# One decoder layer on Trainium2: two token tiles ahead of the expert gathers, the other three beside them

## The reference

```python
mod = silu(c) @ w_ada + b_ada;  sh1, sc1, ga1, sh2, sc2, ga2 = split(mod, 6)
h = rmsnorm(x, g_pre1) * (1 + sc1) + sh1
parts = split(h @ w_in)                      # mLSTM, dilated attention, two gates
branch_a = mlstm(parts, state) @ w_a;  branch_b = attention(parts, caches) @ w_b
merged = sigmoid(parts[14]) * branch_a + sigmoid(parts[15]) * branch_b
x = x + ga1 * rmsnorm(merged @ w_out, g_post1)
h2 = rmsnorm(x, g_pre2) * (1 + sc2) + sh2
q = h2 @ peer_wq                             # 8 heads x 2 halves x 128
# per token and head: top 16 of 128 keys in each half, top 16 of the 256 sums
act = gelu(einsum('td,thkd->thk', h2, u[eidx]))
f = einsum('thk,thkd->td', softmax(sc) * act, v[eidx])   # 16384 experts, rows of 1024
x = x + ga2 * rmsnorm(f, g_post2)
```

## Time and profile before

| | us |
|---|---|
| median of 3 runs | 2613.13 (2599.5 to 2623.63) |
| profiled execution, own time | 2621.62 |
| its span in the profile | 2619.8 |
| TensorE busy | 2230.4 (85%) |
| VectorE busy | 1232.3 (47%) |
| ScalarE busy | 699.8 (27%) |
| GpSimd busy | 733.4 (28%) |
| TensorE clock granted, mean | 0.911 |

### The profile page before, as it was taken

How to read it: one execution, slowest core, us unless ns; L and a number is a source line. 1 busy time by engine, 2 the same in 40 slices (tenths; PEclk the granted TensorE clock), 3 DMA queues, 4 the chain that set the end, 5 groups by cost and what they waited for, 6 DMA issues and landing times.

```text
span 2619.8 us, 24988 instructions
## 1 busy us (share of the span) xinstructions
PE 2230.4 (85%) x9002; PEld 1266.2 (48%) x9002; DVE 1232.3 (47%) x3186; ACT 699.8 (27%) x2118; POOL 733.4 (28%) x694
## 2 busy tenths in 40 slices
PE   6999989988687999988879797978888768687786
PEld 2777438875575777454434343434443323233221
DVE  1000001215223011466766767667676776767764
ACT  2000012232121000233333333333333443333322
POOL 0000001111101000035444353434444444344441
PEclk8999989997676999999999898989999899898889
DMA  6566648978673126089999999999999999999997
GB/s 270 230 256 256 242 144 304 320 288 326 234 263 135 53 73 206 33 331 418 418 417 420 412 420 410 419 405 420 408 417 414 416 420 410 414 415 412 419 414 302
DMA packets 134915, 850.42 MB, mean 325 GB/s; under 512 B 15121, under 2 KB 32817, under 8 KB 52989
## 3 DMA queue, kind: packets, MB, share of 16 engines
q0 software_dynamic: 85760, 691.32, 65.1%
q1 hardware_dynamic: 47740, 154.95, 16.2%
q10 hardware_dynamic: 1290, 2.55, 0.3%
HBM read 836.43 MB, written 99.37 MB: 357 GB/s over the span
## 4 chain that ended last, share of the span: by engine, by line
PE 21%; DVE 17%; DMA 17%; ACT 2%; issue 2%; POOL 1%; ACTq 0%; POOLq 0%
PE ps L1694 17%; DMA pr_ring<-in_uv,pr_idx 17%; DVE pr_ring L1873 4%; PE ps L1643 3%; POOL pr_ring L1602 1%; PE ps L1616 1%; DVE pr_hot L1857 1%; DVE pr_hot L1853 1%; DVE pr_ind L1834 1%; ACT pr_coef L1750 1%; DVE pr_ind L1831 1%; DVE pr_pick L1860 1%; DVE pr_val L1833 1%; DVE pr_rest L1832 1%; DVE pr_val L1830 1%
## 5 line engine op out<-in xcount | busy, mean ns | idle before, releaser
L1694 PE MATMUL ps<-pr_ring,pr_diag 128*128 128x512 f32 (+1 forms) x2304 | 1082.4, 625 | 274.1 <-ACT pr_diag L1754 274.1
L1602 POOL DMA_INDIRECT pr_ring<-in_uv,pr_idx x576 | 661.7, 1149 | 1099.3 <-PE ps L1694 766.0
L1873 DVE CUSTOM_DVE_ANT_0 pr_ring<-pr_ring,h 128x1024 f32<-128x1024 f32 x576 | 690.8, 1224 | 421.5 <-DMA pr_ring<-in_uv,pr_idx 420.2
L1694 PEld LDWEIGHTS ps<-pr_ring,pr_diag 128*128 128x128 f32 (+1 forms) x2304 | 437.5, 195 | 879.9 <-issue 509.2
L1745 ACT ACTIVATE pr_gel<-pr_dots 128x2 f32<-128x2 f32 x288 | 58.3, 202 | 619.1 <-DVE pr_dots L1873 619.0
L1754 ACT ACTIVATE pr_diag<-ident,pr_coef 128x128 f32<-128x128 f32 x512 | 173.5, 386 | 0.0
L1750 ACT ACTIVATE pr_coef<-pr_gel,pr_wgt 128x1 f32<-128x1 f32 x576 | 138.5, 287 | 27.6 <-ACT pr_gel L1745 1.1
L1414 PE MATMUL ps<-trunk,h 128*128 128x288 f32 x512 | 129.5, 413 | 12.6 <-DMA h<-in_w_merge 12.6
L1616 PE MATMUL ps<-trunk,pr_wq 128*128 128x192 f32 (+3 forms) x544 | 131.4, 396 | 0.4 <-ACT trunk L1712 0.4
L430 PE MATMUL ps<-trunk,ap_ring 128*128 128x288 f32 x384 | 126.5, 411 | 2.9 <-PEq L323 2.9
L431 PE MATMUL ps<-trunk,ap_ring 128*128 128x288 f32 x384 | 125.5, 409 | 0.0
(11 more groups left out here) (291 smaller groups left out, 2044.8 us busy)
## 6 DMA issues: line engine op xcount, KB each, us to landing
...
sa_ring<-in_cache SPq DMA_DIRECT2D x24, 1024.0 KB, 7.8
...
sa_ring<-in_kcacheB SPq DMA_DIRECT2D x16, 1024.0 KB, 7.6
...
h<-in_w_merge SPq DMA_DIRECT2D x16, 768.0 KB, 4.3
...
```

The source lines that it names most:

```text
L1602: pool.indirect_dma_start(ring[:, n % RING, :], None, d["uv"], bass.IndirectOffsetOnAxis(ap=idx[:, b % 4, j:j + 1], axis=0)).then_inc(arri ...
L1694: mm = pe.matmul(ps[0:r, bank + half, :], diag[:, n % RING, 0:r], ring[:, n % RING, o:o + CHUNK], start=h == 0 and j == 0, stop=b == FINAL ...
L1873: ins = dve.tensor_tensor_reduce(u, u, e.h2[:, BLOCKS[b][0], :], 1.0, 0.0, ALU.mult, ALU.add, dots[:, n % RING:n % RING + 1])
```

## The change

`merge` now covers only the 256 columns of tiles 0 and 1, and only they are projected, normed and turned ahead of the loop. The 320 columns of tiles 2 to 4 are done inside it: from g = 2 on a unit every three steps (gate, branch, nothing), then eight feature blocks of the output projection, transposed, one every two steps, then 13 steps for each of three tiles (transposes back, the two norms, `turn`). Their weights come a second time, through two slots `side_unit`. The blocks go by two tiles now: tiles 0 and 1 through 8 heads, tiles 2 and 3 through 8 heads, tile 4. So there are 16 rounds of queries, of 256 columns and then of 320, whose weights (1 MB each) have one slot in place of two. The ring of gathers has 8 slots in place of 10.

```diff
-GROUP = 3
+GROUP = 2
 GROUPED = GROUP * P
-BLOCKS = [(i, h) for h in range(PH) for i in range(GROUP)] + [(i, h) for i in range(GROUP, NCH) for h in range(heads_of(i))]
+REST = T - GROUPED
+BLOCKS = ([(i, h) for h in range(PH) for i in range(GROUP)] + [(i, h) for h in range(PH) for i in range(GROUP, PT)]
+          + [(PT, h) for h in range(heads_of(PT))])
...
-QUERY_BANK, SCORE_BANK, SUM_BANK = 0, 1, 2
-
...
+def round_of(b):
+
+    return min(b // 2, ROUNDS - 1)
+
+
+def query_count(r, piece):
+
+    return piece if r == 0 else 4 + 2 * (r - 1) + piece
...
+def query_span(r, piece):
+
+    if r == 0:
+        return slice(piece // 2 * P, (piece // 2 + 1) * P)
+    return slice(0, GROUPED) if r < PH else slice(GROUPED, T)
+
+
...
+def query_piece(g):
+
+    b, q = divmod(g, PER)
+    if b == 0:
+        return (1, q) if q in (0, 1) else None
+    if b > 0 and b % 2 and q in (4, 6) and b // 2 + 2 < ROUNDS:
+        return b // 2 + 2, (q - 4) // 2
+    return None
+
...
-RING = 10
+    sp.dma_start(e.wq[:], d["peer_wq"][h // 2][:, :, o:o + 2 * P]).then_inc(e.wq_ready, 16)
+
+
+def side_merge(g):
+
+    u, step = divmod(g - SIDE_FIRST, 3)
+    return (u, step) if 0 <= u < 2 * KD and step < 2 else None
+
+
+def side_product(g):
+
+    b, step = divmod(g - SIDE_FIRST - 3 * 2 * KD, 2)
+    return b if 0 <= b < KD and step == 0 else None
+
+
+def side_tile(g):
+
+    i, step = divmod(g - SIDE_FIRST - 3 * 2 * KD - 2 * KD, 13)
+    return (i + GROUP, step) if 0 <= i < NCH - GROUP else None
...
+RING = 8
 BATCH = 2
 PER = TOPK // BATCH
+SIDE_FIRST = 2
```

The first gather waits for the two tiles alone, and TensorE's step gets the side work after its values and scores:

```diff
-                        if n == 2:
-                            pool.wait_ge(s_mm, NCH)
-                        if n == 8:
-                            pool.wait_ge(s_h2, NCH)
+                        if n == 0:
+                            pool.wait_ge(s_mm, GROUP)
                         if n >= RING:
                             pool.wait_ge(s_v, n - RING + 1)
...
+                def rest_gate(u):
+                    pe.wait_ge(front.unit_ready[u % 2], 16 * (u // 2 + 1))
+                    if u >= 1:
+                        pe.wait_ge(s_sig, u)
+                    for c in range(KD):
+                        mm = pe.matmul(ps[:, SIDE_BANK, 0:REST], front.unit[:, u % 2, c, :], k.hT[:, c, rest_cols],
+                                       start=c == 0, stop=c == KD - 1)
+                    mm.then_inc(s_gate, 1)
+
+                def rest_branch(u):
+                    if u >= 1:
+                        pe.wait_ge(s_taken, u)
+                    src = k.oaT if u % 2 else k.hmT
+                    for c in range(H):
+                        mm = pe.matmul(ps[:, SIDE_BANK + 1, 0:REST], front.unit[:, u % 2, KD + c, :], src[:, c, rest_cols],
+                                       start=c == 0, stop=c == H - 1)
+                    mm.then_inc(s_branch, 1)
...
@@ -1697,19 +1784,35 @@
                             mm.then_inc(s_v, 1)
                         if q == SCORE and b + 2 < len(BLOCKS):
                             scores(b + 2)
-                        for piece in query_pieces(i, h, q):
-                            query(h + 1, piece)
+                        g = b * PER + q
+                        if query_piece(g):
+                            query(*query_piece(g))
+                        unit = side_merge(g)
+                        if unit and unit[1] == 0:
+                            rest_gate(unit[0])
+                        if unit and unit[1] == 1:
+                            rest_branch(unit[0])
+                        if side_product(g) is not None:
+                            rest_product(side_product(g))
+                        tile = side_tile(g)
+                        if tile and tile[1] == 0:
+                            rest_rows(tile[0])
+                        if tile and tile[1] == 10:
+                            turn(tile[0])
```

SP now walks through the same steps, each load behind the work that frees its slot:

```diff
+                sp.wait_ge(s_q, query_count(1, 0))
+                load_query_weights(sp, d, e, 1)
+                for g in range(PER * FINAL[PT]):
+                    piece = query_piece(g)
+                    if piece and piece[1] == 1 and piece[0] + 1 < ROUNDS:
+                        sp.wait_ge(s_q, query_count(piece[0] + 1, 0))
+                        load_query_weights(sp, d, e, piece[0] + 1)
+                    unit = side_merge(g)
+                    if unit and unit[1] == 1:
+                        u = unit[0] + 2
+                        sp.wait_ge(s_branch, unit[0] + 1)
+                        if u < 2 * KD:
+                            sp.dma_start(front.unit[:, u % 2], d["w_merge"][u]).then_inc(front.unit_ready[u % 2], 16)
+                        else:
+                            sp.dma_start(front.unit[:, u % 2, 0:KD, :], d["w_out_b"][u - 2 * KD]).then_inc(
+                                front.unit_ready[u % 2], 16)
+                    feature = side_product(g)
+                    if feature is not None and feature + 2 < KD:
+                        sp.wait_ge(s_out_mm, feature + 1)
+                        sp.dma_start(front.unit[:, feature % 2, 0:KD, :], d["w_out_b"][feature + 2]).then_inc(
+                            front.unit_ready[feature % 2], 16)
```

```diff
+                def chunk(at):
+                    pe.wait_ge(ready[at], 16)
+                    if at >= 2:
+                        pe.wait_ge(s_part, at - 1)
+                    for step in range(2):
+                        for j in range(4):
+                            c = 2 * j + step
+                            mm = pe.matmul(ps[32 * j:32 * j + 32, at % 2, :], k.cs[:, c, :], w[:, at, c, :],
+                                           start=step == 0, stop=step == 1)
+                    mm.then_inc(s_mm, 1)
+
+                def fold(at):
+                    pe.wait_ge(s_part, at + 1)
+                    for b in range(HALF):
+                        o = (at * HALF + b) * NC
+                        mm = pe.matmul(ps[:, FOLD, o:o + NC], part[:, at, b * P:(b + 1) * P], fold9[:], start=True, stop=True)
+                    mm.then_inc(s_fold, 1)
+
                 pe.wait_ge(s_silu, 1)
-                for w in range(NCK):
-                    pe.wait_ge(ready[w % NR], 16 * (w // NR + 1))
...
+                    for i in range(PT):
+                        pe.transpose(ps[:, TURN + c % 4, i * P:(i + 1) * P], x[:, i, c * P:(c + 1) * P], k.ident[:])
+                    pe.transpose(ps[:, SAMPLE, c * TS:(c + 1) * TS], x[0:TS, PT, c * P:(c + 1) * P],
+                                 k.ident[0:TS, 0:TS]).then_inc(s_tr, 1)
+                pe.wait_ge(s_const, 112)
+                fold(0)
+                fold(1)
+                chunk(2)
+                chunk(3)
+                pe.wait_ge(s_mod, 1)
+                fold(2)
+                fold(3)
 
```

490 lines of the change are left out of this document (266 added, 224 removed).

## The result

| | before | changed |
|---|---|---|
| median, us | 2617.27 (5 runs, 2599.5 to 2623.63) | 2647.46 (5 runs, 2639.13 to 2662.23) |
| ratio | | 1.0161, 95% interval 1.0108 to 1.0214 |
| profiled execution, own time (span) | 2621.62 (2619.8) | 2662.19 (2660.4) |
| TensorE / VectorE busy | 2230.4 / 1232.3 | 2223.2 / 1232.1 |
| clock granted, mean | 0.911 | 0.912 |

What follows compares the result with a forecast made beforehand. TensorE was taken to bound the merge and DMA the expert loop. Terms -145 + 69 + 24 + 27 + 27 + 11 gave +13 us on the profiled 2621.6 us, carried to the median as 2626 us; range 2555 to 2690.

Steps and rivals of the forecast that it cites:

- the gains: All terms ahead of the expert loop (first stage, merge, start of the loop) taken together: -145 us.
- First stage: Start of the kernel: inputs load first, matmuls go side by side, attention begins about 43 us: -19 us (-15 to -24).
- Merge: Ahead of the loop: fewer records of 256 columns per unit, load only just covered: -102 us (-95 to -103).
- Start of the loop: From merge to block 1: first gather goes out earlier, but TensorE waits for query weights: -24 us (-14 to -32).
- Side steps: Loop steps with merge and product work, 7.25 blocks: TensorE becomes the bound, 50.5 us a block: +69 us (+57 to +87).
- The three tiles: Norms and turns of three tiles in the loop, 39 steps: ring stall, queries and VectorE work: +24 us (+11 to +45).
- Ring of 8: Loop to the end of block 33: first gather behind a routing lands 1.3 us late each block: +27 us (0 to +60).
- Query rounds: Eight rounds in odd blocks behind the side work: step 6's query delays a gather, 3.3 us each: +27 us (+10 to +40).
- their weights: Loop: 15 loads of 1 MB query weights where there were 6, 2.5 us each if DMA is full: +11 us (+8 to +20).
- Rival A: Loop: DMA hides nearly all of the added work, faster at 2554 us; chance 0.28.
- Rival B: Loop: only seven gathers under way after each routing, queue empties, 4 us a block, 2708 us; chance 0.29.
- Rival C: Side work: table switches and in-order waits of ScalarE and VectorE show, 42 us on top, 2668 us; chance 0.05.

Runs made afterwards that it cites:

- e3: Kernel before with only the new first stage (modulation in column form, input loads first): 2600.8 us, ratio 0.996 to before.
- e6: Changed kernel with the two queries of a round in steps 2 and 4 instead of 4 and 6: 2621.9 us, ratio 1.005 to before.
- e12: e10 plus round 1's query weights in ring slot 9 and a tile's mean one step later: 2551.2 us, ratio 0.977 to before.
- e10: e9 with the first two loads of side weights issued later, behind the keys: 2566.1 us, ratio 0.982 to before.
- e4: Changed kernel with half of the side work's matmuls left out, all loads kept: 2649.2 us, ratio 1.016 to before.
- e7: Changed kernel without the side weight loads behind the first two units, all matmuls kept: 2645.0 us, ratio 1.012 to before.
- e8: Changed kernel with both half of the side matmuls and the later side weight loads left out: 2622.9 us, ratio 1.003 to before.
- e2: Changed kernel with ten ring slots again instead of eight: 2579.3 us, ratio 0.987 to before.
- e1: Kernel before with one change, gathers going round 8 slots instead of 10: 2712.9 us, ratio 1.040 to before.
- e9: Changed kernel with ten ring slots and the queries moved to steps 2 and 4: 2568.2 us, ratio 0.983 to before.

## Why the prediction came out as it did

The predicted 2626 us lies 21 below the median of 2647.5; the gains were 9 us smaller than the sum said at block 1 (136 for 145), and the costs behind it 18 larger (176 for 158). By the spans, the side steps were put 12 us too high, the three tiles 12 too low, and ring, queries and weights together 19 too low (65 for 84). That the misses partly cancel, and that the median falls 2.5 us inside the forecast's own range, is in part luck. The largest single miss is the ring.

- **First stage, -19:** the mechanism was right; the attention started at 50.16 and not near 43, -11.6, and e3 confirms -12. In e6 and e12, whose transposes ran at the pace of TensorE's upper clock, it started at 43.2 and 42.6. The lead's other 6.5 us are not the change's: kernels with this same first stage had the merge's first load anywhere from 808 to 839 us.
- **Merge, -102:** right. From the first gate to the first product less its wait, 832.05 to 917.12, it takes 85.1 us against the 87 worked out.
- **Start of the loop, -24:** too much by 10. What the step left out was a queue it moved work into: SP issues two more loads of weights at the end of the merge, they take 13.31 us to issue, and TensorE cannot begin the next part before. e10 gives 12.7 us back in the front. So the first gather went out at 977 and not near 965. The landing of round 1's weights was sized well: issued at 994.17, used at 1005.43, 11 us against 10.
- **Side steps, +69 (bounds 57 and 87):** the lower bound was the answer, 48.9 us a block. TensorE was the bound as predicted, at 198 of 200 us and clock 0.99, but DMA stood 1 us below it (e4, e7, e8), so the 50.5 for two near-full engines meeting was not needed. With ten slots it is 48.2.
- **The three tiles, +24:** blocks 8 to 13 cost 35.6, of which the ring accounts for 13 to 16 (e2, e1) where I had counted 1.3 a block, and the place of the queries for 8.8 (e6). What is left, 10 to 14 us, no run takes apart.
- **Ring of 8, +27:** this term was mis-sized, and it explains most of the rest. The 1.3 us for the first gather behind a stall came out on average (blocks 8 to 33 of e1). What failed is what the term put at nothing, the gathers behind it. They are issued some 2 us apart with one or two others under way, and six of them lose another 1.8 us. By the length of the blocks e1 measures 2.4 to 3.0 us, a little less than the two together, since a block of the kernel before already takes 40.9 us where 16 x 2.49 is 39.8. For the 20 blocks 14 to 33 it gives +48.8 where 1.3 gave 26. Why the rate of 2.49 us does not come back at once, the runs do not show. In the side steps I had counted nothing for the ring, nearly rightly: ten slots take 4.5 us from blocks 1 to 7 (e2), though e1, with no side work to hide it, pays 21.
- **Query rounds, +27, and their weights, +11:** right in size, wrong in place, and bound to the ring of 8 (with ten slots the move is worth nothing, e9). With the ring's part taken off by e1, blocks 14 to 27 hold 30.4 us of queries and weights for seven rounds, 4.3 each; predicted 3.3 and part of 11 us in all. The odd blocks were to be longer; it is the even ones (47 against 43), since the delayed gathers belong to the next block's dots.
- **Rival A** (DMA hides nearly all) is out: its point of decision, a landing within 5 us on an idle queue, is missed by e1's 6.1. **Rival B** (the ring runs dry) had the better size for the ring, 2.4 to 3.0 measured of its 4 us a block: the late blocks came out at 43.7, near its 44, the DMA share at 0.96, below its 0.97, and its condition, 1.8 us a block, is met. The total stayed nearer to the forecast than to B's 2708. Over blocks 8 to 33 e1 gives 65 us for the ring, where B had 103 and the forecast 34, and the side steps took 12 us less than either had. I had given the forecast 1.3 because the trace of before showed the two landings of 5.7 and 6.0, and had asked only after the first gather. **Rival C** is out: in e8 all sigmoids, table loads and in-order waits are still there and blocks 1 to 7 stand 10 us above e1, queries included, where C asked 42. The Trainium skill, "ScalarE: Activation LUTs", section "What ACT_TABLE_LOAD costs", adds a drain of 1.38 us to each load (the 2.66 us that the prediction gives stand there); the trace has 59 loads of 1.28 us ahead of the gelu (75.7 us) and the gelu right behind them (load at 995.65, gelu at 996.95), so no drain shows.
